# Differential attention branch: the output norm's inverse taken with tokens on partitions and spread over the features by TensorE inside the next gate's projection

## The chip, the cores and the metric

The kernel runs on one core of one Trainium2 chip. The metric is the device time of one execution in microseconds (us). Lower is better. TensorE (PE) does the matmuls, with its weight loads listed apart (PEld); DVE is VectorE, ACT is ScalarE, POOL is GpSimd, and SP starts the DMAs.

## What is computed

The model is a block of dilated and neighbourhood attention with a feed-forward part, followed by two hybrid layers over 512 latent and 256 context tokens. Each hybrid layer has three branches: latent attention (`mla`), differential attention (`diff`) and sliding-window attention (`swa`). The change touches the end of the differential branch, where the output of each of eight heads (128 features) is normalised over its features, scaled and gated:

```python
def diff_post(o, subln, lam_init):
    b, n = o.shape[:2]
    return (rms_norm(o, subln) * (1.0 - lam_init)).reshape(b, n, DIFF_HEADS * DIFF_V)

# merge_branches: y is a branch's output, z its gate, r the branch
terms.append(jax.nn.sigmoid(gr) * ((y * jax.nn.silu(zr)) @ w_branch[r]))
```

So a head's output is `o / sqrt(mean(o*o) + eps) * subln * (1 - lam_init) * silu(z)`, where the mean is over the 128 features of a token. The first layer also computes the context tokens (768 columns in all), the second one only the 512 latent tokens.

## The kernel before

Everything is kept with features on the 128 partitions and tokens along the free dimension. A weight block of 1024x128 is loaded by SP into `w_raw`, rounded by ACT to `w_high` (`act_high`), and the rest is taken by DVE as `w_low` (`dve_low`). A projection (`split_steps`, `pe_split`) is then, for each of eight 128-row slices, three matmuls: high by high, high by low, low by high. The first layer does this for 512 and then for 256 columns, the second layer for 512 only. A generator "step" is one such trio. `few(steps, n)` takes n of them, so that a projection can be laid between other work.

The `diff` stage runs its eight heads in a loop of seven rounds (`step` in `pe_units`) and an `epilogue` for the last. In each round TensorE does, in this order: the scores of head i with the q, k and v projections of head i+1 laid between them (`pe_scores`), the probability transposes and value products (`pe_values`), the transposes of the next v (`pe_turn_v`), the sums of squares of this head's output (`pe_oss`), and the next head's gate projection (`pe_proj_z`, 24 matmuls of 512 columns and in the first layer 24 of 256). The next round's `pe_scores` opens with a wait for `y`, the finished output of this head.

The chain between the value products and `y` goes through three engines:

- ACT squares the output (`act_osq`, L1539) into `EB` (a part of the tile `probs`).
- TensorE multiplies an all-ones 128x128 block by the squares (`pe_oss`, L1552). This gives the sum over features, already repeated on all 128 partitions, in banks 4 and 6.
- ACT takes the root (L1544) of all 128x512 (and 128x256) numbers, after loading the function table for it.
- DVE inverts them (L1520), multiplies output, `subln` scale and inverse (L1523), and multiplies by the gate into `Y` (L1529), which signals `y`.

DVE then does the gate of the next head: `dve_proj_z` makes `w_low` of the next q weights (L625), waits for ACT's tanh of the gate projection (L1470), and finishes the gate (L1486). After that it takes the maxima of the next head's first scores (L922), ACT takes the exponentials (L890), and only then may the second group of scores overwrite the banks of the first.

After the last head there is no next gate in the stage. The stage `merge` with `r` = 1 follows (L2349 and after): TensorE's first projection there goes to banks 0 and 1, its second waits for `y`, and its third and fourth work on the rounded rows of `Y`. These rows are prepared by ACT and DVE (`y_round`, `y_rows`, `y_split`) once `y` is there, since both engines pass a fence at the end of the `diff` stage.

The same shape that the change brings in is already used for the latent norms in the stage `pre`: `pe_latent` sums squares with tokens on partitions, ACT and DVE work on a 128x6 tile (L2229, L2235), and `pe_spread` (L2062) multiplies a broadcast column by the identity to put the inverses back along the free dimension. Every fp32 matmul of `ones` or `ident` shows as two passes in the trace.

Of the kernel before, what the change touches and what calls it, by code (L numbers as in the profile page):

```python
# [20 lines left out]
ALU = mybir.AluOpType  # L21
# [97 lines left out]
def plan():  # L119
# [24 lines left out]
    def add(s, **kw):  # L144
        for k, v in kw.items():
# [3 lines left out]
            "rl_wide k_roped v_turned pt_act pt_dve rl_mm transposed o_done o_sq o_ss o_rs y bias merged up_ev gelu f_high f_low y_low y_high y_round m_high m_low out_ev ctx_in mod_copy mod_sum qk_high qk_low").split()  # L149
# [5 lines left out]
    for i, s in enumerate(st):  # L155
# [13 lines left out]
        elif k == "units":  # L169
# [12 lines left out]
            if s["name"] == "diff":  # L182
                add(s, vt_in=n, vt_mm=n, v_ev=n, z_ev=n, tanh=n, swap_q=64 * n, swap_k=64 * n, roped=2 * n, q_out=n, o_sq=n, o_ss=n, o_rs=n)
                add(s, h=2, k_out=2)
# [38 lines left out]
def program(nc, w, out, scratch_t5, scratch_na, rows_t5, rows_na):  # L223
    stages, totals = plan()
    ctx = ExitStack()
    with ctx:
# [1038 lines left out]
        def pe_proj_z(pe, s, t, u, i):  # L1265
            name, ui = s["name"], s["unroll"]
            if s["first"]:
                return
            if name == "mla":

                pe.wait_ge(S["roped"], cnt(s, "roped", t, ui, u + 1))
                pe_split(pe, s, t, 2, u, 128, tgroups(2, s["cq"]))
            elif name == "diff":

                pe.wait_ge(S["rope_in"], cnt(s, "rope_in", t, ui, u + 1))
                pe_split(pe, s, t, 4, 3, 128, tgroups(2, s["cq"]))
# [213 lines left out]
        def dve_output(dve, s, t, u, i, sub):  # L1490
# [25 lines left out]
            if name == "diff":  # L1516

                dve.wait_ge(S["o_rs"], cnt(s, "o_rs", t, per, po + 1))
                for lo, n, b in groups:
                    v.reciprocal(EB[:, 0, lo:lo + n], EB[:, 0, lo:lo + n])  # L1520
                v.drain()
                for lo, n, b in groups:
                    v.scalar_tensor_tensor(out=EB[:, 0, lo:lo + n], in0=bank(b, n), scalar=GS[:, s["l"]:s["l"] + 1],  # L1523
                                           in1=EB[:, 0, lo:lo + n], op0=ALU.mult, op1=ALU.mult)
                v.drain()
            for lo, n, b in groups:
                src = EB[:, 0, lo:lo + n] if name == "diff" else PS[r, 512 * b:512 * b + n]
                dst = Y[r, bass.ds(i, 1), lo:lo + n].rearrange("p a t -> p (a t)") if not isinstance(i, int) else Y[r, i, lo:lo + n]
                last = v.scalar_tensor_tensor(out=dst, in0=src, scalar=0.5, in1=Z[r, lo:lo + n], op0=ALU.mult, op1=ALU.mult)  # L1529
# [3 lines left out]
        def act_osq(act, s, t, u, i):  # L1533
# [9 lines left out]
            for lo, n, b in groups:  # L1543
                last = act.activation(EB[:, 0, lo:lo + n], bank(b - 1, n), ACT.Sqrt, scale=1.0 / 128, bias=EPSB[:, :])  # L1544
            last.then_inc(S["o_rs"], 1)

        def pe_oss(pe, s, t, u, i):

            pe.wait_ge(S["o_sq"], cnt(s, "o_sq", t, s["unroll"], u + 1))
            groups = [(0, LAT, 5)] + ([(LAT, CTX, 7)] if s["cq"] else [])  # L1550
            for lo, n, b in groups:
                last = mm(bank(b - 1, n), ones[:, :], EB[:, 0, lo:lo + n], start=True, stop=True)  # L1552
            last.then_inc(S["o_ss"], 1)

# [51 lines left out]
        def pe_units(pe, s):  # L1606
# [88 lines left out]
            def step(t, u, i):  # L1695
# [5 lines left out]
                if name == "diff":  # L1701
                    pe_scores(pe, s, t, u, i, 0, qkv_steps(t, u, i), n_side)
                    pe_values(pe, s, t, u, i, 0)
                    pe_turn_v(pe, nxt, t, u)
                    pe_oss(pe, s, t, u, i)
                    pe_proj_z(pe, nxt, t, u, i + 1)
                    return
# [564 lines left out]
        def pe_stage(pe, s):  # L2272
# [65 lines left out]
            elif k == "merge":  # L2338
# [18 lines left out]
                else:  # L2357
# [3 lines left out]
                    pe_split(pe, s, 0, 4, 0, 128, tgroups(0, s["ctx"]))  # L2361
# [747 lines left out]
```

## Time and profile before

| what | value |
|---|---|
| runs (us) | 3863.46, 3870.72, 3872.88 |
| median | 3870.72 |
| the profiled execution | 3862.4, its span 3860.6 |
| mean granted TensorE clock | 0.975 of 2.4 GHz |
| PE busy | 3640.3 (94%) |
| DVE busy | 2043.3 (53%) |
| ACT busy | 1426.3 (37%) |

The profiled execution took 1.8 us more than its span. It lies 8.3 us below the median of the runs shown. The `diff` heads of the first layer lie at about 1515 to 1960 us, those of the second layer at about 3010 to 3380 us. A bracket at the end of a row gives the idle time before it and what ended it.

### The profile page before, as it was taken

How to read it: one execution, taken by the hardware profiler on the slowest of the kernel's cores; microseconds unless marked ns; L12 is line 12 of the kernel's file. 1: busy time of each engine (PE TensorE's matmuls, PEld its weight loads, DVE VectorE, ACT ScalarE, POOL GpSimd, SP SyncE). 2: the span in 40 equal slices, each digit the busy share in tenths (PEclk: the TensorE clock that was granted, in tenths of full speed). 3: DMA queues.
4: the chain of work that ended last, by engine and by line, in shares of the span. 5: the costliest groups of instructions: out<-in, count | busy, mean ns of one | idle time of the engine just before them, and what ended most of it. 6: DMA issues, size and time to landing. Idle time of an engine off the chain costs nothing.

```text
span 3860.6 us, 54876 instructions
## 1 busy us (share of the span) xinstructions
PE 3640.3 (94%) x20163; PEld 2824.5 (73%) x20163; DVE 2043.3 (53%) x3393; ACT 1426.3 (37%) x2534; POOL 265.7 (7%) x196
## 2 busy tenths in 40 slices
PE   6998989999799999999999999998999999999998
PEld 4665768878667788777778776886668777676666
DVE  4555346553545533777733555244553567645544
ACT  3433233323333322444431545122333344524532
POOL 0000000000011001111000100000110221001100
PEclk9998989999799999999999999997999999999999
DMA  7553325543101122211112111211113222131122
GB/s 257 158 138 95 92 85 165 167 139 109 50 21 30 27 65 58 52 48 50 44 49 57 42 28 50 66 55 49 29 37 93 61 64 55 49 92 51 42 77 79
DMA packets 506585, 286.93 MB, mean 74 GB/s; under 512 B 48129, under 2 KB 485469, under 8 KB 506438
## 3 DMA queue, kind: packets, MB, share of 16 engines
q1 hardware_dynamic: 485979, 264.60, 24.6%
q10 hardware_dynamic: 20459, 20.36, 1.8%
q8 instruction: 94, 1.54, 0.2%
q14 instruction: 53, 0.43, 0.0%
HBM read 269.05 MB, written 10.32 MB: 72 GB/s over the span
## 4 chain that ended last, share of the span: by engine, by line
issue 90%; PE 3%; POOL 3%; POOLq 2%; DVE 1%; ACT 0%; DVEq 0%; ACTq 0%
PE ps L629 3%; POOLq L1385 2%; POOL qT L1384 2%; POOL qT L1386 1%; POOL y_and_merged L1384 1%; DVEq L3028 0%; DVE w_low L625 0%; PE ps L2472 0%; DVE probs L911 0%; PE ps L1070 0%; POOLq L212 0%; DVE h_low L2270 0%; DVE y_low L2803 0%; ACT w_high L615 0%; DVE y_and_merged L3005 0%
## 5 line engine op out<-in xcount | busy, mean ns | idle before, releaser
L629 PE MATMUL ps<-h_high,w_high 128*128 128x512 f32 (+1 forms) x3432 | 1285.0, 374 | 45.9 <-DVE w_low L625 24.5
L629 PE MATMUL ps<-h_low,w_high 128*128 128x512 f32 (+1 forms) x3432 | 1246.7, 363 | 0.0
L629 PE MATMUL ps<-h_high,w_low 128*128 128x512 f32 (+1 forms) x3432 | 1243.7, 362 | 0.0
L629 PEld LDWEIGHTS ps<-h_high,w_high 128*128 128x128 f32 x3432 | 652.7, 190 | 209.5 <-issue 60.5
L625 DVE TENSOR_TENSOR w_low<-w_raw,w_high 128x1024 fp32r<-128x1024 f32 x374 | 463.3, 1239 | 590.2 <-ACT w_high L615 568.0
L629 PEld LDWEIGHTS ps<-h_high,w_low 128*128 128x128 f32 x3432 | 652.7, 190 | 103.3
L629 PEld LDWEIGHTS ps<-h_low,w_high 128*128 128x128 f32 x3432 | 654.0, 191 | 93.7 <-issue 3.1
L615 ACT ACTIVATE w_high<-w_raw 128x1024 fp32r<-128x1024 f32 x374 | 387.8, 1038 | 641.1 <-PE ps L629 549.4
L890 ACT ACTIVATE probs<-ps,neg_max 128x768 f32<-128x768 f32 (+1 forms) x240 | 194.8, 815 | 407.0 <-DVE neg_max L922 406.8
L629 PE MATMUL ps<-probsT,v 128*128 128x512 f32 (+4 forms) x736 | 285.7, 557 | 14.0 <-DVE probsT L1133 8.7
L922 DVE TENSOR_REDUCE neg_max<-ps 128x1 f32<-128x768 f32 (+1 forms) x240 | 196.7, 847 | 162.9 <-PE ps L629 152.9
L629 PE MATMUL ps<-y_high,w_high 128*128 128x512 f32 (+1 forms) x640 | 230.4, 360 | 8.1 <-issue 6.5
L629 PE MATMUL ps<-k_high,q_high 64*128 64x256 f32 (+4 forms) x784 | 181.5, 385 | 57.1 <-DVE neg_max L908 19.2
L629 PE MATMUL ps<-y_high,w_low 128*128 128x512 f32 (+1 forms) x640 | 229.8, 359 | 0.0
L890 ACT ACTIVATE probs<-probs,neg_max 128x512 f32<-128x512 f32 (+1 forms) x192 | 145.6, 758 | 172.0 <-DVE neg_max L914 123.1
L629 PE MATMUL ps<-y_low,w_high 128*128 128x512 f32 (+1 forms) x544 | 194.9, 358 | 0.0
L629 PEld LDWEIGHTS ps<-k_high,q_high 64*128 64x128 f32 (+1 forms) x784 | 88.9, 186 | 128.8 <-issue 31.5
L1019 PEld LDWEIGHTS ps<-ident,probs 128*128 128x128 f32 x832 | 101.6, 141 | 94.8 <-issue 85.3
L629 PE MATMUL ps<-k_low,q_high 64*128 64x256 f32 (+4 forms) x784 | 153.1, 323 | 0.0
L629 PE MATMUL ps<-k_high,q_low 64*128 64x256 f32 (+4 forms) x784 | 152.8, 322 | 0.0
L2807 DVE SCALAR_TENSOR_TENSOR probs<-probs,ps 128x512 f32<-128x512 f32 x88 | 51.9, 613 | 189.6 <-PE ps L629 189.6
L1133 DVE COPY probsT<-ps 128x512 f32<-128x512 f32 x112 | 73.2, 654 | 142.8 <-PE ps L1019 142.3
(250 smaller groups left out, 4158.6 us busy)
## 6 DMA issues: line engine op xcount, KB each, us to landing
w_raw<-in_w_in SPq DMA_DIRECT2D x436, 256.0 KB, 3.2
y_and_merged<-in_w_mod SPq DMA_DIRECT2D x96, 256.0 KB, 3.2
w_raw<-in_w_branch SPq DMA_DIRECT2D x96, 256.0 KB, 3.0
w_raw<-in_w_up SPq DMA_DIRECT2D x88, 256.0 KB, 4.3
y_and_merged<-in_w_ada SPq DMA_DIRECT2D x64, 256.0 KB, 3.2
w_raw<-in_w_out SPq DMA_DIRECT2D x48, 256.0 KB, 3.0
w_raw<-in_w_down SPq DMA_DIRECT2D x44, 256.0 KB, 3.2
y_and_merged<-in_w_ada SPq DMA_DIRECT2D x4, 2048.0 KB, 17.2
```

What stands on the lines that cost most here:

```text
L615: act.activation(WR[:, k, 0:nk], WRAW[:, k, 0:nk], ACT.Copy).then_inc(s_high, 1)
L625: nc.vector.tensor_tensor(WL[:, k, 0:nk], WRAW[:, k, 0:nk], WR[:, k, 0:nk].bitcast(F32), ALU.subtract).then_inc(s_low, 1)
L629: return nc.tensor.matmul(*a, **kw)
L890: act.activation(it["dst"], src, ACT.Exp, bias=NM[:, idx:idx + 1], accum_out=SL[:, idx:idx + 1]).then_inc(S["exped"], 1)
L922: v.tensor_reduce(NM[:, idx:idx + 1], src, AXX, ALU.max, negate=True).then_inc(S["maxed"], 1)
L1019: last = nc.tensor.transpose(PS[:, b:b + 128], tile, ident[:, :])
L1133: nc.vector.tensor_copy(PT[:, which, 0:m], PS[:, b:b + m]).then_inc(S["pt_dve"], 1)
L1384: g.tensor_tensor(x, x, cos, ALU.mult)
L1385: g.drain()
L1386: g.tensor_tensor(x, x, swapped, ALU.add).then_inc(S["roped"], 1)
L2807: v.scalar_tensor_tensor(out=d, in0=d, scalar=1.0, in1=p, op0=ALU.add, op1=ALU.mult)
```

## The change

ACT squares the output as before. `pe_oss` now makes each 128-token slice of the squares the stationary operand and streams two columns of `ones`, so that the sums come out with tokens on partitions, one column per slice: six matmuls in the first layer and four in the second, all in bank 4, in place of one matmul per 512 or 256 columns. ACT's root and DVE's inverse then work on `LT2[:, 0, 0:nt]`, a 128x6 or 128x4 tile. A new function `pe_osp` waits for the inverse (`o_ri`) and multiplies each of its columns, broadcast to 128x128, by the identity, into banks 4 and 6. It stands inside the next gate's projection, after five of its trios. For the last head it stands inside the first projection of the `merge` stage, also after five trios. DVE, meanwhile, multiplies output, scale and gate, then waits for `o_sp`, and makes the last multiplication with the spread inverse read from the banks.

```diff
-        def pe_proj_z(pe, s, t, u, i):
+        def pe_proj_z(pe, s, t, u, i, outer=None):
...
-                pe_split(pe, s, t, 4, 3, 128, tgroups(2, s["cq"]))
+                gate = split_steps(pe, s, t, 4, 3, 128, tgroups(2, s["cq"]))
+                if outer is not None:
+                    few(gate, 5)
+                    pe_osp(pe, s, t, outer)
+                for _ in gate:
+                    pass
...
                 dve.wait_ge(S["o_rs"], cnt(s, "o_rs", t, per, po + 1))
-                for lo, n, b in groups:
-                    v.reciprocal(EB[:, 0, lo:lo + n], EB[:, 0, lo:lo + n])
-                v.drain()
+                nt = tiles_of(cq)
+                v.reciprocal(LT2[:, 0, 0:nt], LT2[:, 0, 0:nt]).then_inc(S["o_ri"], 1)
                 for lo, n, b in groups:
                     v.scalar_tensor_tensor(out=EB[:, 0, lo:lo + n], in0=bank(b, n), scalar=GS[:, s["l"]:s["l"] + 1],
-                                           in1=EB[:, 0, lo:lo + n], op0=ALU.mult, op1=ALU.mult)
+                                           in1=Z[:, lo:lo + n], op0=ALU.mult, op1=ALU.mult)
                 v.drain()
+
+                dve.wait_ge(S["o_sp"], cnt(s, "o_sp", t, per, po + 1))
             for lo, n, b in groups:
                 src = EB[:, 0, lo:lo + n] if name == "diff" else PS[r, 512 * b:512 * b + n]
+                by = bank(b - 1, n) if name == "diff" else Z[r, lo:lo + n]
...
-                last = v.scalar_tensor_tensor(out=dst, in0=src, scalar=0.5, in1=Z[r, lo:lo + n], op0=ALU.mult, op1=ALU.mult)
+                last = v.scalar_tensor_tensor(out=dst, in0=src, scalar=0.5, in1=by, op0=ALU.mult, op1=ALU.mult)
...
-            for lo, n, b in groups:
-                last = act.activation(EB[:, 0, lo:lo + n], bank(b - 1, n), ACT.Sqrt, scale=1.0 / 128, bias=EPSB[:, :])
-            last.then_inc(S["o_rs"], 1)
+            nt = tiles_of(cq)
+            sums = bank(4, 2 * nt).rearrange("p (a e) -> p a e", e=2)
+            act.activation(LT2[:, 0, 0:nt], sums[:, :, 0], ACT.Sqrt, scale=1.0 / 128, bias=EPSB[:, :]).then_inc(S["o_rs"], 1)
...
-            groups = [(0, LAT, 5)] + ([(LAT, CTX, 7)] if s["cq"] else [])
-            for lo, n, b in groups:
-                last = mm(bank(b - 1, n), ones[:, :], EB[:, 0, lo:lo + n], start=True, stop=True)
+            for tt in range(tiles_of(s["cq"])):
+                last = mm(bank(4, 2, 2 * tt), EB[:, 0, 128 * tt:128 * tt + 128], ones[:, 0:2], start=True, stop=True, skip_group_check=True)
             last.then_inc(S["o_ss"], 1)
+
+        def pe_osp(pe, s, t, u):
+
+            pe.wait_ge(S["o_ri"], cnt(s, "o_ri", t, s["unroll"], u + 1))
+            for tt in range(tiles_of(s["cq"])):
+                ps = bank(4, 128, 128 * tt) if tt < 4 else bank(6, 128, 128 * (tt - 4))
+                last = mm(ps, LT2[:, 0, tt:tt + 1].to_broadcast([128, 128]), ident[:, :], start=True, stop=True, skip_group_check=True)
+            last.then_inc(S["o_sp"], 1)
...
-                    pe_proj_z(pe, nxt, t, u, i + 1)
+                    pe_proj_z(pe, nxt, t, u, i + 1, u)
...
-                    pe_split(pe, s, 0, 4, 0, 128, tgroups(0, s["ctx"]))
+                    gate = split_steps(pe, s, 0, 4, 0, 128, tgroups(0, s["ctx"]))
+                    if s["r"] == 1:
+                        few(gate, 5)
+                        pe_osp(pe, stages[s.index - 1], 7, 0)
+                    for _ in gate:
+                        pass
```

## Rows read from the trace of the kernel before

**Rows 1.** The page: busy time of each engine, with its share of the span.

```profile
PE 3640.3 (94%) x20163; PEld 2824.5 (73%) x20163; DVE 2043.3 (53%) x3393; ACT 1426.3 (37%) x2534; POOL 265.7 (7%) x196
```

**Rows 2.** PE's waits, 1550 to 1930 us, first layer: total, times, longest.

```profile
PE ps L629 <- ACT probs L890: 8.8, 11, 1.8
PE ps L629 <- DVE y_and_merged L1529: 2.3, 7, 0.3
```

**Rows 3.** PE's waits, 3040 to 3355 us, second layer.

```profile
PE ps L629 <- DVE y_and_merged L1529: 4.1, 7, 0.6
```

**Rows 4.** Timeline of one head's end, first layer: start, duration, engine, instruction.

```profile
1559.31 1.56 PE L629 MATMUL ps<-probs,ones 128*128 128x512 f32 x4 [0.31 <-ACT probs L1539]
...
1560.94 0.40 PE L629 MATMUL ps<-h_low,w_high 128*128 128x512 f32 x1
...
1561.99 4.96 DVE L1520 RECIPROCAL probs<-probs 128x512 f32<-128x512 f32 x2 [1.79 <-ACT probs L1544]
...
1567.03 1.14 DVE L1523 SCALAR_TENSOR_TENSOR probs<-ps,subln,probs 128x512 f32<-128x512 f32 x2
...
1568.36 1.03 DVE L1529 SCALAR_TENSOR_TENSOR y_and_merged<-probs,y_and_merged 128x512 f32 x2 [0.19 <-issue]
...
1568.95 0.28 PE L629 MATMUL ps<-h_high,w_low 128*128 128x256 f32 x1
...
1569.33 1.28 ACT L1470 ACT_TABLE_LOAD   x1 [6.42 <-PE ps L629]
...
1569.53 0.50 PE L629 MATMUL ps<-k_high,q_high 64*128 64x512 f32 x2 [0.31 <-DVE y_and_merged L1529]
...
1576.05 0.51 PE L629 MATMUL ps<-k_high,q_high 64*128 64x512 f32 x2 [0.16 <-ACT probs L890]
```

**Rows 5.** Timeline of one head's end, second layer.

```profile
3140.66 1.12 PE L629 MATMUL ps<-probs,ones 128*128 128x512 f32 x2
...
3141.86 0.39 PE L629 MATMUL ps<-h_low,w_high 128*128 128x512 f32 x1
...
3146.87 0.39 PE L629 MATMUL ps<-h_high,w_low 128*128 128x512 f32 x1
...
3147.01 0.69 DVE L1529 SCALAR_TENSOR_TENSOR y_and_merged<-probs,y_and_merged 128x512 f32 x1 [0.18 <-issue]
...
3147.84 0.51 PE L629 MATMUL ps<-k_high,q_high 64*128 64x512 f32 x2 [0.59 <-DVE y_and_merged L1529]
```

**Rows 6.** Timeline of the latent norms (stage `pre`): the spread, two sums, the small tiles.

```profile
1054.25 0.19 DVE L2235 RECIPROCAL latent_rstd_rows<-latent_rstd_rows 128x6 f32<-128x6 f32 x1 [3.84 <-ACT latent_rstd_rows L2229]
...
1064.74 1.50 PE L629 MATMUL ps<-ident,latent_rstd_rows 128*128 128x128 f32 x12
...
1066.31 0.40 PE L629 MATMUL ps<-h_low,w_high 128*96 128x512 f32 x1
...
1076.61 2.74 PE L629 MATMUL ps<-ones,probs 128*128 128x2 f32 x24
```

**Rows 7.** Stretches: busy time per engine, granted clock (PEclk), DMA share, GB/s.

```profile
1077.00:1079.50 2.50, 2.34 (x21) 2.26 (x21) 1.98 (x4) 0.12 (x1) 0.00 (x0) 1.00 0.00 0
1079.80:1083.00 3.20, 3.20 (x5) 0.93 (x5) 1.20 (x3) 0.00 (x0) 0.00 (x0) 0.50 0.01 3
1557.00:1560.50 3.50, 3.11 (x16) 1.87 (x15) 3.03 (x4) 2.10 (x3) 0.00 (x0) 1.00 0.43 129
```

**Rows 8.** Timeline of the first layer's last head and the `merge` stage after it.

```profile
1938.48 1.56 PE L629 MATMUL ps<-probs,ones 128*128 128x512 f32 x4 [0.96 <-ACT probs L1539]
...
1940.61 0.39 PE L629 MATMUL ps<-h_low,w_high 128*128 128x512 f32 x1
...
1947.43 1.03 DVE L1529 SCALAR_TENSOR_TENSOR y_and_merged<-probs,y_and_merged 128x512 f32<-128x512 f32 x2
...
1951.59 0.47 PE L629 MATMUL ps<-h_high,w_high 128*128 128x512 f32 x1 [2.73 <-DVE w_low L625]
...
1964.08 0.77 PE L629 MATMUL ps<-y_high,w_high 128*128 128x512 f32 x1 [3.92 <-issue]
```

More of the change, by code:

```diff
@@ L148, in plan @@
     keys = ("h n square added square_mm rstd scaled high low_row lat_sq lat_ss lat_rs lat_ri lat_sp lat_n rinv spread fin down_ev x_t mm_ev rope_in rope_mm roped q_mm k_mm k_out q_out kv_ev kv_low vt_in vt_mm v_ev z_ev tanh swap_q swap_k z_scaled scores maxed exped normed "
-            "rl_wide k_roped v_turned pt_act pt_dve rl_mm transposed o_done o_sq o_ss o_rs y bias merged up_ev gelu f_high f_low y_low y_high y_round m_high m_low out_ev ctx_in mod_copy mod_sum qk_high qk_low").split()
+            "rl_wide k_roped v_turned pt_act pt_dve rl_mm transposed o_done o_sq o_ss o_rs o_ri o_sp y bias merged up_ev gelu f_high f_low y_low y_high y_round m_high m_low out_ev ctx_in mod_copy mod_sum qk_high qk_low").split()
     for k in keys:
@@ L182, in plan @@
             if s["name"] == "diff":
-                add(s, vt_in=n, vt_mm=n, v_ev=n, z_ev=n, tanh=n, swap_q=64 * n, swap_k=64 * n, roped=2 * n, q_out=n, o_sq=n, o_ss=n, o_rs=n)
+                add(s, vt_in=n, vt_mm=n, v_ev=n, z_ev=n, tanh=n, swap_q=64 * n, swap_k=64 * n, roped=2 * n, q_out=n, o_sq=n, o_ss=n, o_rs=n, o_ri=n, o_sp=n)
                 add(s, h=2, k_out=2)
```

## Prediction

> **What bounds the kernel now.** I read the page first, then PE's waits, then the timeline at the end of a head, and last the stages that already use the new shape. The page says that PE is busy for 94% of the span [rows 1], so an instruction added to PE counts in full unless it falls into one of PE's own waits. The waits tell what the present norm costs: in the first layer PE waits for `y` 7 times, 2.3 us in all [rows 2], and in the second layer 7 times, 4.1 us [rows 3]. DVE's 4.96 us of inverses look dear in the timeline, but they lie beside the gate projection [rows 4]. PE's second gate matmul starts at 1560.94, its last at 1568.95, and the scores that need `y` at 1569.53 with 0.31 us of waiting. That wait, not the 4.96 us, is what a faster norm can give back.
>
> In the first layer even that is not free. After the gate projection another chain runs: ACT loads its tanh table (1569.33), takes the tanh, DVE finishes the gate and takes the maxima, ACT the exponentials, and only at 1576.05 may PE start the second group of scores, 0.16 us after it could have [rows 4]. The chain starts at the end of the gate projection and not at `y`. If the first group starts 0.3 us earlier, PE waits 0.3 us longer before the second. So I credit nothing for the wait for `y` in the first layer. In the second layer the gate projection is 24 matmuls instead of 48 while the scores' side work (nine steps of 512 columns) covers this chain (the view lists no wait for L890 there), so its wait [rows 3, 5] comes back in full.
>
> **The sums** (`pe_oss`). First layer: 6 matmuls, so 12 passes, with two moving columns each, for 2 matmuls of 512 and 256 columns. Before, 1.63 us pass from the first pass to the second gate matmul (1559.31 to 1560.94) [rows 4]. For 12 short passes the spread of the latent norm shows 1.57 us between the same points (1064.74 to 1066.31), and 24 two-column sums take 2.74 us, so the pace of 0.11 us a pass holds for them too [rows 6]. That is -0.06 us a head. Second layer: 8 passes, 1.57 - 4 x 0.11 = 1.13 us, against 1.20 (3140.66 to 3141.86) [rows 5]: -0.07. Shorter streams gain nothing, because each pass has a weight block of its own.
>
> **The spread** (`pe_osp`) is new work on PE, in the middle of a projection that PE does without a gap. Without it the second matmul after 1064.74 would have come 0.23 us later, the spacing of 512-column matmuls ((3146.87 - 3141.86) / 22) [rows 5]. It came 1.57 us later [rows 6], so 12 passes cost 1.34 us and 8 passes 0.90. This is the dear part. It can't be less than the passes' own pace, and can be more by one wait bubble of about 0.1 us. No cover is assumed.
>
> **Root, inverse, products.** ACT's root falls from 768 columns to 6. Its table load stays, and ends at about the time of the last sum. DVE's inverses fall from 4.96 us [rows 4] to 0.19 [rows 6]. All of this is off PE. The new wait of PE for `o_ri` comes five trios, 15 x 0.23 = 3.4 us, behind the sums. Root and inverse work on 128x6 numbers by then, 0.19 us for the inverse [rows 6] and about as much for the root, with the signals some 1 us, so it costs nothing. If that cover were gone, what stands behind it is the rest of the gate projection, and behind that the scores. DVE's new wait for `o_sp` holds back `w_low` of the next q weights (L625), the gate and the maxima. But `y` now comes at about 1.57 + 3.0 + 0.23 + 1.34 + 0.3 us plus DVE's last product of 1.03, so 7.5 us after the first sum, against 10.1 before (1568.36 + 1.03) [rows 4]. All of them are still earlier than today.
>
> **Steady heads, on PE.** First layer: 7 x (1.34 - 0.06) = +9.0 us. Second layer: spread 7 x 0.90 = 6.3, sums 7 x -0.07 = -0.5, wait for `y` -4.1 [rows 3]: +1.7 us.
>
> **The ends of the two stages.** Here no gate of a next head follows and `y` is on the path: PE waits 2.73 us at 1951.59 for a `w_low` that DVE makes after `y`, and 3.92 us at 1964.08 for the rows that are rounded after `y` [rows 8]. The spread itself fits into these waits. Before, the last product starts 8.95 us behind the first sum (1938.48 to 1947.43). The change of stage puts the second matmul 0.5 us later than in a steady head (2.13 us for 1.63) [rows 8]. After: 1.57 + 0.5, 13 further matmuls at 0.23 (3.0), 0.23 to the first spread, 1.34, and about 0.3 until DVE reads it, 6.9 in all. The whole chain moves forward by 2.0 us, and PE's wait of 3.92 us takes that as a gain. Second layer: before 6.35 us (3140.66 to 3147.01) [rows 5], after 1.13 + 0.5 + 3.0 + 0.23 + 0.90 + 0.3 = 6.1: -0.2 us.
>
> **The granted clock.** In the latent norm PE did 24 two-column passes and waited a little, at a granted 1.00 (2.4 GHz), and then stood at 0.50 (1.2 GHz) for over 3.20 us [rows 7]. So PE can be busy by its records and still lose its clock when hardly a column streams. The end of a head held 1.00 [rows 7], but 1.56 us of it were the wide `ones` matmuls [rows 4] that the change removes. What is left before the gate is six v transposes, a wait of 0.31, and the sums. At the first layer's last head the wait is 0.96 us [rows 8] and no transposes precede it, so I count on one fall there: half of 3.2 us, +1.6. For steady heads the price of a fall lies between 0 and 1.6 us each. I take 0, since their sums are 1.3 us and not 2.7, with a full-rate projection right behind.
>
> The Trainium skill has a rule that speaks against this. "TensorE: Matmul & The Clock Gate", Part 4 (PE-mode transpose), says that transposes don't count as work for the clock in the way other matmuls do. By it the v transposes, the wait and the sums would all be rest to the clock, and it would fall at every head of both layers. No row here isolates a transpose from other matmuls, so the trace doesn't settle it. It is rival three.
>
> **The sum.** 9.0 + 1.7 - 2.0 - 0.2 + 1.6 = +10.1 us. Against the profiled execution that is 3862.4 + 10.1 = 3872.5. It ran 8.3 us below the median, so against the median of 3870.7 I forecast 3880.8, rounded 3881 (+0.26%).
>
> **Rivals.**
> 1. Chance 0.25: the clock falls in the first layer's steady heads too. For: the wide matmuls that kept PE streaming are gone, and the latent norm shows the fall after such sums [rows 7]. Against: the sums are half as long here. If about half of the seven heads fall: 3.5 x 1.6 = +5.6, 3886. If all: +11.2, 3892.
> 2. Chance 0.12, not slower: at the stage ends the shorter wait keeps the clock that today is lost behind it. The place is the `merge` stage. PE restarts at 1964.08 after 3.92 us of idleness [rows 8], and the wait would be 1.9 us now. If three low stretches of 3.2 us around the two stage ends go (-4.8) and the fall that I count on (+1.6) doesn't come, 8.5 - 4.8 = +3.7: 3874.4, no measurable change. It decides from the point where the remaining idleness is short enough for the clock to stay. The second layer's wait hardly shortens, which speaks against it.
> 3. Chance 0.05: the clock sees the stretch of transposes, wait and sums as rest, and every steady head of both layers falls: 14 x 1.6 = 22.4 on top of 10.1, 3903.
> 4. Chance 0.04: faster. The wait for `y` and what queues behind it on DVE is dearer than PE's idle rows show, for example a late `w_low` for the q projection. This would have to give back over 3 us a head in the first layer, where all of PE's listed waits together are 11.1 us [rows 2].
> 5. Chance 0.04: the change doesn't do what it says. The wait for `o_ri` stalls the gate projection. At 1 us a head this is +14: 3895.
>
> **How the numbers follow.** The forecast has 0.50. I give each case about 4 us either way, since the runs shown spread by 9.4 us. Leaving out rival three, rival four and the upper ends of one and five, the range is 3870 to 3894. About 0.3% (11.6 us) is what a measurement of this kernel can tell from no change: below 3859 is faster, above 3882.3 slower. The forecast lies just inside, so 0.17 of its 0.50 goes to slower. With 0.20 of rival one, 0.05, 0.04 and nothing of two, slower is 0.46, faster 0.04, the same 0.50.
>
> **What the profile after would show.** The spread as 12 (8) passes over 1.3 (0.9) us in mid-gate; no wait of PE at L1529; in the first layer a longer wait for ACT's L890 before the second score group; the first layer's head longer by 1.3 us, the second layer's by 0.2; PE's 3.92 us wait down to about 2. A PEclk of 0.50 right behind the sums, in heads that had 1.00, would speak for rival one or three. A head period that doesn't grow in the first layer would prove the main step wrong.

## The result and the profile after

The changed kernel takes 3873.69 us (median of 20 executions, 3863.34 to 3883.68). The kernel before takes 3863.65 us on the same chip (20 executions, 3855.36 to 3872.88). The ratio is 1.0027, 95% interval 1.0019 to 1.0034, so +10.0 us, between +7 and +13. The forecast was +10.1 us, and its 3881 us is 7 us above the measured time because the three runs it was laid on had a median 7 us above that of the twenty.

The page of the changed kernel, busy time of each engine:

```profile
span 3867.6 us, 55388 instructions
...
PE 3656.5 (95%) x20435; PEld 2851.5 (74%) x20435; DVE 1977.4 (51%) x3385; ACT 1415.8 (37%) x2526; POOL 266.1 (7%) x196
```

Against [rows 1] DVE has lost 65.9 us and ACT 10.5 us, while PE has gained 16.2 us. The kernel is slower. The engine that was relieved was not the one that sets the end.

The timeline at the end of a first-layer head (start, duration, engine, instruction), to be laid beside [rows 4]:

```profile
1609.03 1.50 PE L629 MATMUL ps<-ones,probs 128*128 128x2 f32 x12 [0.31 <-ACT probs L1546]
...
1610.57 0.27 ACT L1552 ACTIVATE latent_rstd_rows<-ps,eps 128x6 f32<-128x6 f32 x1 [0.29 <-PE ps L629]
...
1610.71 0.39 PE L629 MATMUL ps<-h_low,w_high 128*128 128x512 f32 x1
...
1610.87 0.19 DVE L1525 RECIPROCAL latent_rstd_rows<-latent_rstd_rows 128x6 f32<-128x6 f32 x1 [0.95 <-ACT latent_rstd_rows L1552]
...
1613.91 1.50 PE L629 MATMUL ps<-ident,latent_rstd_rows 128*128 128x128 f32 x12
...
1615.57 1.02 DVE L1536 SCALAR_TENSOR_TENSOR y_and_merged<-probs,ps 128x512 f32 x2 [3.49 <-PE ps L629]
...
1620.28 0.50 PE L629 MATMUL ps<-k_high,q_high 64*128 64x512 f32 x2
...
1620.45 1.28 ACT L1475 ACT_TABLE_LOAD   x1 [8.66 <-PE ps L629]
...
1627.14 0.49 PE L629 MATMUL ps<-k_high,q_high 64*128 64x512 f32 x2 [0.52 <-ACT probs L890]
```

The product that makes `y` now starts 6.54 us behind the first sum instead of 9.05. The scores no longer wait for it: the row at 1620.28 has no bracket. Still they start 11.25 us behind the first sum and not 10.22, because 12 passes of spread lie in front of them. The second group starts at 18.11 instead of 16.74, and its wait for the exponentials has grown from 0.16 to 0.52 us.

PE's waits in the first layer (1545 to 1935 us: total, times, longest), to be laid beside [rows 2]:

```profile
PE ps L629 <- ACT probs L890: 12.2, 16, 2.3
PE ps L629 <- ACT probs L1546: 2.1, 7, 0.3
```

The 2.3 us for `y` are gone, and the wait for L890 went from 8.8 to 12.2 us, of which about 0.5 belong to the last head (its longest wait went from 1.8 to 2.3 us). The wait only changed its name. In the second layer the 4.1 us for `y` [rows 3] are gone and nothing has taken their place.

The granted clock is where the traces hold something that the working did not have. Stretches of the changed kernel (length, busy time per engine, then PEclk, DMA share, GB/s):

```profile
1606.50:1610.00 3.50, 3.11 (x22) 2.37 (x20) 3.02 (x4) 1.87 (x3) 0.00 (x0) 1.00 0.29 87
...
1907.00:1909.50 2.50, 2.50 (x13) 1.95 (x14) 0.41 (x1) 0.00 (x0) 0.00 (x0) 0.50 0.63 163
...
1934.00:1937.00 3.00, 3.00 (x7) 1.70 (x8) 0.25 (x1) 0.26 (x1) 0.00 (x0) 0.50 0.00 0
...
1947.50:1950.50 3.00, 3.00 (x8) 2.32 (x8) 0.79 (x2) 1.18 (x2) 0.00 (x0) 0.50 0.00 0
...
3361.00:3363.50 2.50, 2.50 (x7) 1.41 (x6) 0.00 (x0) 0.39 (x1) 0.00 (x0) 0.50 0.00 0
```

And the kernel before at the places that answer to the second (1907), third (1934) and fourth (1947.5) of them:

```profile
1904.00:1907.50 3.50, 3.50 (x21) 2.77 (x17) 2.90 (x7) 1.88 (x4) 0.00 (x0) 1.00 0.57 150
1931.00:1935.00 4.00, 4.00 (x21) 2.42 (x20) 1.38 (x2) 0.60 (x1) 0.00 (x0) 1.00 0.00 0
...
1942.00:1946.00 4.00, 4.00 (x20) 3.34 (x19) 4.00 (x2) 0.78 (x1) 0.00 (x0) 1.00 0.00 0
```

The steady heads keep 1.00 (2.4 GHz), the sums and v transposes at 1606.5 included. The last head of the first layer runs at 0.50 (1.2 GHz) in two places where it did not before: behind the wait for its second score group, and in its last value products. The fall right behind its sums (1947.5) was forecast.

Where the time went, by stretches of the traces. The marks are the first pass of each head's sums and, at the stage ends, the first matmul on rows rounded from `y`. "Steady" is from the first head's mark to the seventh's, "end" from there to the rounded rows. All in us, of one profiled execution each:

| kernel | steady, layer 1 | end, layer 1 | steady, layer 2 | end, layer 2 | rest |
|---|---|---|---|---|---|
| before | 327.3 | 77.44 | 267.2 | 61.23 | 3127.4 |
| changed | 335.9 | 81.34 | 268.8 | 62.79 | 3118.7 |
| spread twice | 343.9 | 84.24 | 274.4 | 64.20 | 3120.8 |
| one tile spread | 329.2 | 79.33 | 264.8 | 59.78 | 3128.8 |
| short inverse | 327.3 | 72.67 | 263.1 | 57.29 | 3121.7 |
| early product | 327.4 | 76.23 | 263.2 | 59.65 | 3123.4 |
| early product, second run | 327.3 | 76.24 | 263.1 | 61.29 | 3125.0 |
| new at the ends | 327.3 | 76.68 | 267.2 | 62.16 | 3127.8 |
| new in steady heads | 335.9 | 81.81 | 268.8 | 61.41 | 3122.6 |
| spread after two trios | 335.9 | 79.32 | 268.8 | 59.04 | 3122.5 |
| combined | 327.4 | 76.03 | 263.1 | 59.37 | 3126.5 |
| combined, second run | 327.5 | 74.66 | 263.1 | 58.11 | 3125.9 |
| wide sums, idle spread | 335.7 | 81.75 | 268.6 | 62.65 | 3123.4 |
| wide sums, idle stream | 335.5 | 82.02 | 268.6 | 63.07 | 3126.2 |

The steady columns repeat to 0.2 us between kernels that share the code (six head periods each, so 8.6 / 6 = 1.44 us a head in the first layer and 0.26 in the second). The rest, which no edit touches, lies anywhere between 3119 and 3129 us. So a head's price is read from the steady columns, and the total from the comparisons of medians.

### The profile page after: what moved, and what is told of

Same layout as the page of the kernel before. It is cut to its first block, busy times and chain, and to the rows that moved or that the text cites. A ratio compares the mean times of both kernels' runs of the same rounds, so it can differ in the third digit from the quotient of the medians.

```text
span 3867.6 us, 55388 instructions
## 1 busy us (share of the span) xinstructions
PE 3656.5 (95%) x20435; PEld 2851.5 (74%) x20435; DVE 1977.4 (51%) x3385; ACT 1415.8 (37%) x2526; POOL 266.1 (7%) x196
## 4 chain that ended last, share of the span: by engine, by line
issue 90%; PE 3%; POOL 3%; POOLq 2%; DVE 1%; ACT 0%; DVEq 0%; ACTq 0%
PE ps L629 3%; POOLq L1390 2%; POOL qT L1389 2%; POOL qT L1391 1%; POOL y_and_merged L1389 1%; DVEq L3047 0%; PE ps L2491 0%; DVE w_low L625 0%; DVE probs L911 0%; PE ps L1070 0%; POOLq L212 0%; DVE h_low L2284 0%; DVE y_low L2822 0%; ACT w_high L615 0%; ACT y_high L2583 0%
## 5 line engine op out<-in xcount | busy, mean ns | idle before, releaser
L890 ACT ACTIVATE probs<-ps,neg_max 128x768 f32<-128x768 f32 (+1 forms) x240 | 194.5, 814 | 404.7 <-DVE neg_max L922 404.5
L629 PE MATMUL ps<-k_high,q_high 64*128 64x256 f32 (+4 forms) x784 | 180.7, 386 | 48.9 <-DVE neg_max L908 15.9
L890 ACT ACTIVATE probs<-probs,neg_max 128x512 f32<-128x512 f32 (+1 forms) x192 | 145.6, 758 | 169.9 <-DVE neg_max L914 121.3
```

The costliest lines, as they stand in the source:

```text
L629: return nc.tensor.matmul(*a, **kw)
L890: act.activation(it["dst"], src, ACT.Exp, bias=NM[:, idx:idx + 1], accum_out=SL[:, idx:idx + 1]).then_inc(S["exped"], 1)
```

## The experiments

**The spread doubled.** In the changed kernel:

```diff
-            for tt in range(tiles_of(s["cq"])):
+            for tt in 2 * list(range(tiles_of(s["cq"]))):
                 ps = bank(4, 128, 128 * tt) if tt < 4 else bank(6, 128, 128 * (tt - 4))
```

> The changed kernel, with the spread's matmuls issued twice (24 passes for 12 in the first layer, 16 for 8 in the second; the output stays the same). Theory A (PE is the bound in mid-gate, each pass costs its own 0.11 us): +1.34 us a steady head in the first layer and +0.90 in the second, 7 x 2.24 = +15.7 us against the changed kernel, and the head periods go from 56.00 to 57.3 and from 44.80 to 45.7 us. Theory B (the passes lie in slack of the head, and the 10 us that the change costs come from the new wait or from what it moved on DVE): under 3 us more, head periods within 0.3 us.

Measured: 3890.7 us, 1.0076 (1.0062 to 1.0090) of the kernel before, +28.2 us against it and so about +18 against the changed kernel's +10.0. The timeline of two heads' sums with the spread of the first:

```profile
1610.59 1.50 PE L629 MATMUL ps<-ones,probs 128*128 128x2 f32 x12 [0.31 <-ACT probs L1546]
...
1615.46 2.84 PE L629 MATMUL ps<-ident,latent_rstd_rows 128*128 128x128 f32 x24
...
1667.92 1.28 PE L629 MATMUL ps<-ones,probs 128*128 128x2 f32 x10 [0.31 <-ACT probs L1546]
```

The head takes 57.33 us for 56.00, so 12 further passes cost 1.33 us. In the second layer it takes 45.73 for 44.80, so 8 cost 0.93. Theory B (slack) is out.

**One tile spread.** The same loop over `(0,)`.

> The changed kernel with the spread of the first token tile alone (2 passes for 12 and for 8); the inverse norms of the other tiles are left out, DVE reads what stands in the banks. Sums, root, inverse, the wait and the products stay. Theory A: 10 passes less in the first layer and 6 in the second, 7 x (1.12 + 0.67) = -12.5 us against the changed kernel, so some 2 to 3 us below the kernel before; head periods 54.9 and 44.1 us. Theory B: as the changed kernel, within 3 us.

Measured: 3862.95 us, 1.0001 (0.9992 to 1.0010), +0.4 us against the kernel before and so about 10 us less than the changed kernel. That is less than the 12.5 expected. The steady heads did what was expected of them (54.9 and 44.1 us). The four columns of the table put this kernel 15.7 us below the changed one and 0.1 below the kernel before, which fits its +0.4. So what doesn't fit is the total of the changed kernel, and the part on the prediction comes back to it. The rows that carry the head:

```profile
1612.95 1.50 PE L629 MATMUL ps<-ones,probs 128*128 128x2 f32 x12 [0.31 <-ACT probs L1546]
...
1617.84 0.38 PE L629 MATMUL ps<-ident,latent_rstd_rows 128*128 128x128 f32 x2
...
1667.84 1.39 PE L629 MATMUL ps<-ones,probs 128*128 128x2 f32 x11 [0.31 <-ACT probs L1546]
```

54.89 us for 56.00: 0.11 us a pass, the pace of [rows 6]. With 2, 12 and 24 passes the head takes 54.9, 56.0 and 57.3 us, a straight line.

**The inverse cut short.** In the kernel before:

```diff
-                for lo, n, b in groups:
-                    v.reciprocal(EB[:, 0, lo:lo + n], EB[:, 0, lo:lo + n])
+                v.reciprocal(EB[:, 0, 0:6], EB[:, 0, 0:6])
                 v.drain()
```

> The kernel before with DVE's inverses over 6 columns instead of 768 and 512; the inverse of the other tokens' norms is left out. Nothing is added to PE. This prices the delay of y by itself. Theory A: nothing in the first layer's steady heads, -4.1 us (the wait for y) in the second layer's, and at the ends of the two stages the last product starts some 5 us (3.3 us) earlier, of which PE's waits can give back at most 3.9 and about 2: -6 to -10 us against the kernel before. Theory C (DVE's 5 us a head delay more than PE's idle rows show, through low parts and maxima queued behind them): -1 us or more in each of the seven heads of the first layer too, so -15 us and beyond.

Measured: 3843.91 us, 0.9960 (0.9946 to 0.9973), -18.6 us. That is more than theory A gave and in the range of theory C, but C's mechanism is not there: the steady heads of the first layer stay at 54.55 us (327.3 in the table). The second layer's give 4.1 us by the table, as counted, and the four columns together -12.8 us; the medians' interval is -10 to -21. The rest is at the ends, where A was too cautious. At the first layer's end the last product starts 4.17 us behind the first sum, not 8.95:

```profile
1936.88 1.56 PE L629 MATMUL ps<-probs,ones 128*128 128x512 f32 x4 [0.96 <-ACT probs L1538]
...
1939.56 0.19 DVE L1519 RECIPROCAL probs<-probs 128x6 f32<-128x6 f32 x1 [4.39 <-ACT probs L1543]
...
1941.05 1.03 DVE L1528 SCALAR_TENSOR_TENSOR y_and_merged<-probs,y_and_merged 128x512 f32<-128x512 f32 x2
...
1957.70 0.47 PE L629 MATMUL ps<-y_high,w_high 128*128 128x512 f32 x1 [2.09 <-issue]
```

The rounded rows come 20.82 us behind the first sum instead of 25.60: 4.78 us for a product that is 4.78 us earlier. PE's waits for `w_low` and for the rounded rows [rows 8] were both waits for `y`, 6.65 us together, and the forecast of this run allowed 3.9 for this end. The ends together give 8.7 us by the table. Those are the places where an early `y` pays.

**The product taken early.** In the kernel before, DVE waits for the squares only:

```diff
+                dve.wait_ge(S["o_sq"], cnt(s, "o_sq", t, per, po + 1))
+                for lo, n, b in groups:
+                    v.scalar_tensor_tensor(out=EB[:, 1, lo:lo + n], in0=bank(b, n), scalar=GS[:, s["l"]:s["l"] + 1],
+                                           in1=Z[:, lo:lo + n], op0=ALU.mult, op1=ALU.mult)
                 dve.wait_ge(S["o_rs"], cnt(s, "o_rs", t, per, po + 1))
...
-                    v.scalar_tensor_tensor(out=EB[:, 0, lo:lo + n], in0=bank(b, n), scalar=GS[:, s["l"]:s["l"] + 1],
-                                           in1=EB[:, 0, lo:lo + n], op0=ALU.mult, op1=ALU.mult)
...
-                src = EB[:, 0, lo:lo + n] if name == "diff" else PS[r, 512 * b:512 * b + n]
+                src = EB[:, 1, lo:lo + n] if name == "diff" else PS[r, 512 * b:512 * b + n]
+                by = EB[:, 0, lo:lo + n] if name == "diff" else Z[r, lo:lo + n]
```

> The kernel before with its wide sums and inverses, and no spread, but DVE takes the product of output, weight and gate while PE sums, into the other exponential buffer, and only the last product stands behind the inverses. The output stays the same. y comes 1.1 us (first layer) or 0.7 us (second layer) earlier at no cost to PE. Theory A: nothing in the first layer's steady heads (PE then waits longer for the exponentials), the wait for y of 0.59 us a head gone in the second layer, about -4 us, and -1 to -2 at the stage ends: -5 to -6 us against the kernel before. Theory D (the earlier product collides with something on DVE, since it holds the queue from the squares on): no gain or a loss of some us.

Measured: 3856.12 us, 0.9983 (0.9974 to 0.9992), -6.4 us. The same kernel ran once more beside the combined one:

> The same kernel as the one with the early product alone, beside the combined one in one comparison: -6.5 us against the kernel before, as measured and as its trace adds up (steady heads of the second layer -4.0, ends -1.2 and -1.6).

Measured: 3855.34 us, 0.9981 (0.9972 to 0.9990), -7.3 us. The timeline of a second-layer head of the first of these runs, beside [rows 5]:

```profile
3090.93 1.13 PE L629 MATMUL ps<-probs,ones 128*128 128x512 f32 x2
...
3091.80 0.74 DVE L1520 SCALAR_TENSOR_TENSOR probs<-ps,subln,y_and_merged 128x512 f32<-128x512 f32 x1
...
3092.90 3.35 DVE L1525 RECIPROCAL probs<-probs 128x512 f32<-128x512 f32 x1 [0.36 <-ACT probs L1546]
...
3096.44 0.69 DVE L1531 SCALAR_TENSOR_TENSOR y_and_merged<-probs 128x512 f32 x1 [0.19 <-issue]
...
3097.46 0.50 PE L629 MATMUL ps<-k_high,q_high 64*128 64x512 f32 x2
```

The product lies beside the sums, the last product starts 5.51 us behind the first sum (6.35 before), and the scores have no wait in front of them. The whole 4 us that the second layer had to give come back without an instruction on PE. Theory A holds, D falls.

**The two halves of the change.** One kernel takes the new scheme for the last head of each layer alone, the other for the seven steady heads alone. In the changed kernel's code, with the old lines kept for the other case (the second kernel returns the opposite):

```diff
+        def new_norm(i):
+            return (isinstance(i, int) and i == 7)
...
+            if name == "diff" and not new_norm(i):
...
+            if name == "diff" and new_norm(i):
```

`pe_osp` is then called from `merge` only, or from the rounds only.

> The kernel before in the seven steady heads of each layer (wide sums, inverses on DVE, no spread), the new scheme for the last head of each layer alone. Theory A: the steady heads keep 54.55 and 44.53 us; the last product of the stage ends comes as in the changed kernel, the third merge split 25.1 us and 19.3 us behind the first sum instead of 25.6 and 19.6: 0 to -1 us against the kernel before. Theory F (the two low-clock stretches in the first layer's last head, 17 and 45 us behind the sums of the seventh head, come from the narrow sums and the shorter first score group of that head; the one right behind the sums of the last head from those sums): the first two are gone here, the third is there. Theory G (they are a matter of where in the stream an execution happens to stand): no pattern.

> The other half: the new scheme in the seven steady heads of each layer, the kernel before for the last head of each layer. Theory A: periods 56.00 and 44.80 us, 7 x (1.43 + 0.27) = +11.9 us, third merge split at 25.6 and 19.6 us: +12 us against the kernel before, and with the two extra low-clock stretches (theory F: they are there, since the seventh head's sums are narrow) about +15. Theory G: no pattern in the low-clock stretches. Together with the run of the other half it also says whether the two halves add up to the +10 us of the whole change.

Measured: 3862.40 us, 0.9993 (0.9984 to 1.0002), and 3874.16 us, 1.0027 (1.0017 to 1.0037). That is -0.2 and +11.5 us, together +11.3 for the whole's +10.0. The loss is all in the steady heads. In the first layer the low stretches show a pattern, so theory G is out there. The kernel with the old steady heads has none in the first layer's last head. The one with the new has one at 17.5 us behind the seventh head's sums, longer than in the changed kernel (the third score group comes 25.3 us behind those sums for 23.7, and 20.9 without a fall). The fall right behind the last head's sums is there where those sums are narrow (at 1.3 us) and not where they are wide. That fits theory F, but F named two things at once, the narrow sums of the steady heads and their length. The kernels with idle work below separate them. In the second layer no pattern shows. Its last head has a low stretch in the kernel with the old steady heads (3349) and none in the one with the new. Over all fourteen profiled executions four of seven with longer steady heads have one there, and three of the seven others. There theory G stands.

**The spread after two trios.** In the changed kernel, both calls:

```diff
-                    few(gate, 5)
+                    few(gate, 2)
```

> The changed kernel with the spread after two trios of gate matmuls instead of five (first layer: from 2.8 us behind the first sum instead of 4.9). Theory A: PE doesn't wait for the inverse even so (it is written 2.0 us behind the first sum), the steady heads stay at 56.00 and 44.80, and at the stage ends the last product starts 2.1 us earlier (more where the trios ran at the low clock): -2 to -5 us against the changed kernel. Rival H: the inverse is late by some 0.5 us and PE stalls in each of the 14 steady heads: +7 us.

Measured: 3864.77 us, 1.0005 (0.9996 to 1.0014), +2.1 us against the kernel before, 8 less than the changed kernel's +10.0 and more than expected.

```profile
1672.35 0.19 DVE L1525 RECIPROCAL latent_rstd_rows<-latent_rstd_rows 128x6 f32<-128x6 f32 x1 [0.95 <-ACT latent_rstd_rows L1552]
...
1673.32 0.94 PE L629 MATMUL ps<-ident,latent_rstd_rows 128*128 128x128 f32 x7
```

The inverse is there 0.8 us before the spread starts, even so, and the steady columns of the table don't move (rival H is out). The ends give 2.0 and 3.8 us, 5.8 by the table, where some 1.6 of the 3.8 are the low stretch at 3361 that this execution lacks. What the medians show beyond that no stretch of the traces explains. Five trios were more cover than the wait for `o_ri` needed.

**The combined kernel.** Early product and wide sums in the steady heads, new scheme after two trios for the last heads. It ran twice.

> The early product on DVE in the steady heads with wide sums (no work added to PE), and the new scheme with the spread after two trios for the last head of each layer alone. Theory A: the early product's gain in the steady heads of the second layer (7 x 0.67 = -4.7, and -0.8 in its last period), and at the stage ends the last product starts at about 5.0 us behind the first sum instead of 8.95 (first layer) and 4 to 4.5 instead of 6.35 (second): -3 and -2. Together about -10 us against the kernel before, -4 against the early product alone. Rival I (the narrow sums cost the clock at the stage ends): -8 or less gain.

> The same kernel as the combined one. Its trace adds up to -7.3 us against the kernel before, 0.5 us less than the early product alone, while the first comparison gave -11.8 and -6.4. Theory J: the stage ends' narrow sums buy nothing, since the low-clock stretch behind them takes back what the earlier product gives: within 3 us of the early product alone. Rival: they buy another 5 us that one profiled execution each doesn't show.

Measured: 3850.86 us, 0.9962 (0.9948 to 0.9975), and in the second comparison 3844.75 us, 0.9958 (0.9944 to 0.9971), with the early product alone at 0.9981 (0.9972 to 0.9990) beside it. So -12 and -18 us against the kernel before. Theory J is not borne out, since the combined kernel is 10.6 us faster by the medians of that comparison. The intervals don't overlap. By the traces of these two the ends give 1.6 + 3.2 = 4.8 us of it, and 1.6 of that is a low stretch in the second layer's last head (3344) that only one of the early product's two executions has. So the order of the two is measured, its size not. The first end of the second run:

```profile
1939.70 1.57 PE L629 MATMUL ps<-ones,probs 128*128 128x2 f32 x12 [0.96 <-ACT probs L1563]
...
1944.22 1.59 PE L629 MATMUL ps<-ident,latent_rstd_rows 128*128 128x128 f32 x12
...
1945.85 1.02 DVE L1553 SCALAR_TENSOR_TENSOR y_and_merged<-probs,ps 128x512 f32<-128x512 f32 x2 [3.04 <-PE ps L629]
...
1962.50 0.47 PE L629 MATMUL ps<-y_high,w_high 128*128 128x512 f32 x1 [1.36 <-issue]
```

The last product starts 6.15 us behind the first sum, not the 5.0 expected, since the trios in between run at the low clock:

```profile
1941.50:1944.00 2.50, 2.47 (x6) 2.04 (x7) 1.21 (x3) 1.69 (x3) 0.00 (x0) 0.50 0.00 0
```

In the first run that stretch lasted on through 1949, and the end took 1.4 us longer (76.03 for 74.66). This is rival I at work, at some 1 to 3 us. It does not eat the gain. This version beats both kernels.

**What brings the low clock into the last head.** Two kernels with the wide sums of before, in which PE does idle work in the middle of each steady gate, once ACT has read the sums and written the roots:

```diff
+                    few(gate, 5)
+                    pe_extra(pe, s, t, outer)
...
+        def pe_extra(pe, s, t, u):
+            pe.wait_ge(S["o_rs"], cnt(s, "o_rs", t, s["unroll"], u + 1))
+            for tt in range(tiles_of(s["cq"])):
+                ps = bank(4, 128, 128 * tt) if tt < 4 else bank(6, 128, 128 * (tt - 4))
+                mm(ps, LT2[:, 0, tt:tt + 1].to_broadcast([128, 128]), ident[:, :], start=True, stop=True, skip_group_check=True)
```

The second has in place of the last two lines:

```diff
+                mm(bank(4), WR[:, raw_slot(s, t, 4, 3), tt, 0:128], HR[:, tt, 0:512], start=True, stop=True)
```

> The kernel before (wide sums, 768 and 512 inverses on DVE) with the spread's matmuls as idle work in the middle of the gate of the seven steady heads: they go into the sums' banks after ACT has read them, and nobody reads them. It is the spread without anything else of the change. Theory A: first layer, the gate ends 1.34 us later and everything behind it, period 54.55 + 1.34 = 55.9 us; second layer, 0.90 less the wait for y of 0.66 which the longer gate covers, 44.53 + 0.24 = 44.8 us; so 7 x 1.58 = +11 us against the kernel before from the steady heads. For the two low-clock stretches in the first layer's last head two theories: F1, they come from the narrow sums of the steady heads: none here, and the last period stays near 52 us. F2, they come from the head being longer, whatever its sums: they are here, and the last period is near 56 us (another +3 to +4 us).

> As the kernel with wide sums and an idle spread, but in place of the spread's 12 (8) narrow passes PE does 6 (4) more matmuls of 512 columns like those of the gate, into the same bank, which nobody reads: 6 x 0.23 = 1.4 us a head in the first layer, 4 x 0.23 = 0.9 in the second. Theory A: the time is that of the PE work whatever its kind, periods 55.9 and 44.8 us, +11 us against the kernel before from the steady heads. For the two low-clock stretches of the first layer's last head: F2, the longer head brings them, whatever fills it: they are here and the last period is near 56 us. F3, the narrow passes in the middle of the gate bring them: not here, and the last period is 52 us.

Measured: 3873.63 us, 1.0028 (1.0016 to 1.0040), +11.0 us, and 3873.19 us, 1.0025 (1.0016 to 1.0034), +9.7 us. Each reproduces the loss of the whole change, without narrow sums and without a changed norm. The steady heads take 55.95 and 55.91 us in the first layer, and 44.77 and 44.76 us in the second. The stretches of the kernel with the idle spread, then of the one with the idle stream:

```profile
1909.00:1912.00 3.00, 1.82 (x8) 1.13 (x7) 2.75 (x5) 1.66 (x3) 0.00 (x0) 1.00 0.36 102
1913.00:1919.00 6.00, 5.92 (x21) 4.63 (x22) 3.47 (x8) 1.90 (x5) 0.00 (x0) 0.50 0.32 87
```

```profile
1913.00:1915.50 2.50, 2.50 (x14) 1.97 (x11) 0.76 (x1) 0.00 (x0) 0.00 (x0) 0.50 0.74 190
...
1940.50:1943.00 2.50, 2.50 (x7) 1.42 (x6) 0.00 (x0) 0.54 (x1) 0.00 (x0) 0.50 0.00 0
```

The falls in the first layer's last head are there with either filling, so F2 holds, F1 and F3 fall: they go with the longer head. All seven kernels whose first-layer steady heads take 54.9 us or more have the fall at 17 to 20 us behind the seventh head's sums, and none of the five at 54.55 has, in seven profiled executions. The shortest of the seven, with one tile spread, is longer by 0.3 us only. It isn't the wait in front of it either. PE waits 2.26 us for the exponentials there in the early product's kernel too and then runs on at full rate, while in the kernel with the idle spread the same wait is followed by a half-rate start:

```profile
1900.59 0.49 PE L629 MATMUL ps<-k_high,q_high 64*128 64x512 f32 x2 [2.26 <-ACT probs L890]
```

```profile
1913.08 0.79 PE L629 MATMUL ps<-k_high,q_high 64*128 64x512 f32 x2 [2.26 <-ACT probs L890]
```

Why the same wait costs the clock in one and not in the other stays open.

## Why the prediction was right, point by point

- **PE is the bound, and the cover is none.** Right. The spread starts in mid-gate 4.88 us behind the first sum, about as counted (1.57 + 3.4), and its passes show in the head one for one: 1.33 us for 12 by doubling, against 1.34 counted, and 0.93 for 8, against 0.90. The kernel with the idle spread makes the whole +11 us by it alone.
- **The sums.** Next to nothing, as counted, but with the other sign. First sum to second gate matmul took 1.68 us for 1.63 before, +0.05 and not -0.06. In the second layer it was +0.03 and not -0.07. Together with the spread's small surplus the first layer's head grew by 1.44 us for the 1.28 counted, the second layer's by 0.26 for 0.24.
- **The wait for `y`.** Right in both layers. In the first it turned into the wait for L890, and the short inverse, which takes 5 us out of DVE's chain, left that head at 54.55 us. In the second the 4.1 us came back in full, in three kernels by three different means (the new scheme, the short inverse, the early product).
- **The first stage end.** The net was right, the parts also: -2.0 and +1.6 for a fall behind the sums, -0.4 in all. Measured, the rounded rows come 25.07 us behind the first sum for 25.60, -0.5. The fall is seen at 1947.5, and the spread starts at 6.87 us instead of the 5.3 counted, which is the price of the fall. With the chain that much later, PE's wait for the rounded rows went from 3.92 to 3.4 us, not to 2. Its wait of 2.73 us for `w_low` is gone, and the spread and the slow trios stand in its place. The second end: -0.2 counted, -0.3 measured. The count took its 6.35 us from a steady head; in the last head itself it was 6.25 us before and is 5.93 now.
- **The falls in the last heads.** Missed. Two in the first layer's last head and one in the second layer's (3361) lengthen their periods from 51.84 to 56.27 us and from 41.64 to 43.51, of which the ordinary growth of a head is 1.4 and 0.3, so 4.6 us are the falls. The prediction put them at nothing, since it looked for falls only behind the narrow sums. The second layer's was also seen in one of the two runs of the early product and of the combined kernel, and in the kernel with the new scheme at the ends alone, so it is no certain part of the change. The first layer's two are.
- **The total.** By the four columns of the table the change costs 8.6 + 3.9 + 1.6 + 1.6 = 15.7 us in the profiled execution, by the medians 10.0 (7 to 13). The rest of the program was 8.7 us shorter in that one execution, 6.3 of it ahead of the first mark. Three other kernels with the longer steady heads (new in steady heads, idle spread, idle stream) measure 11.5, 11.0 and 9.7 us where their columns give 14.7, 15.5 and 15.9. The kernels with the spread doubled and after two trios measure 28.2 and 2.1 us where theirs give 33.5 and 9.9. So 3 to 8 us are missing from the total in each. One tile spread shows no such gap. The rest averages 3123.3 us in the seven executions with longer heads and 3125.4 in the other seven, within a spread of 10 us, so the traces don't say where these us are given back, or whether they are chance. The steady term is about right by itself, 7 x 1.44 + 7 x 0.26 = 11.9 us for 10.7 counted. That the total met the forecast to 0.1 us is luck: 1.2 us more in the steady heads and 4.6 of falls were not counted, and something that is not settled took them back.
- **The rivals.** One (falls in the steady heads) did not come, nor two, since the low stretches at the ends did not go. Three did not come: the transposes, the wait and the sums at 1606.5 keep 1.00. The Trainium skill ("TensorE: Matmul & The Clock Gate", Part 4, PE-mode transpose) says that transposes don't count as work for the clock in the way other matmuls do. No run here isolates a transpose, but whatever they count for, it cost no steady head its clock. Four: DVE's queue held nothing beyond the idle rows in the steady heads, as the short inverse shows; what `y` was worth more was at the ends. Five: the wait for `o_ri` has 2.9 us to spare, and still 0.8 with two trios.

## What to carry to other kernels

Before work is moved to the engine that sets the end, read how long that engine really waits for the result: here 0.3 and 0.6 us a head, against 1.3 and 0.9 us of new passes. Read also what it waits for next, since in the first layer even the 0.3 us only went over into another wait. A result that is late on another engine is first made earlier by taking out of its chain what doesn't depend on it; the early product gave back all that the steady heads had to give and cost PE nothing. The places where lateness does pay are the ends of a stage, where no next head covers it, and the dear scheme can be used there alone. How early it comes decides: after five trios it gave nothing there (-0.2 us), after two trios it made the combined kernel the fastest of those that leave nothing out.

## What the runs showed of the hardware that I had not expected

- **A fall of the clock can be moved by work far ahead of it.** In the first layer's last head, 1.4 us more in each of the heads before puts PE at 1.2 GHz behind a wait of 2.26 us that costs no clock with shorter heads, whether the added work is narrow passes or full 512-column streams. The second layer's last head shows no such tie.
- **In the first layer's last head narrow sums behind a wait of 0.96 us lose the clock, the wide ones do not.** That is so in all fourteen executions, seven with the one and seven with the other. Behind a wait of 0.31 us and the v transposes the narrow ones kept it in every steady head, and in the second layer's last head they kept it behind a wait of 0.69 us.
- **A small matmul's price does not shrink with its columns.** Passes of 2 and of 128 columns, each with a weight block of its own, take the same time (12 in 1.50 us, about 0.11 us for each further one). So narrowing the streams of the sums from 512 and 256 columns to 2, with a block for each slice, saved no time (1.68 us for 1.63 until the second gate matmul). That the weight block sets this pace is argued, not shown: no kernel here reused one.
